# Reordering the mixers of the first block: the 16-token tile second, output slots divided by tokens, rotations and value turn moved up

## What is computed

```
z = h @ w_in[l]
c_q, c_kv, k_pe, rq, rk, rv, rg = jnp.split(z, split_idx, axis=-1)
y_mla = mla_mixer(c_q, c_kv, k_pe, ...)       # latent attention, 4 heads of 128
y_ret = retention_mixer(rq, rk, rv, rg, ...)  # retention, 4 heads of 128
y = jnp.concatenate([y_mla, y_ret], axis=-1) @ w_out[l]
h_res = h_res + y
```

```
bounds = [0] + [N_META + BLOCK * j for j in range((L - N_META) // BLOCK + 1)]   # 0, 16, 144, 272
s = einsum('bqhd,bkhd->bhqk', qb, kb) * scale;  s = where(causal, s, -1e30)
p = softmax(s);  o = p @ vb                      # then rms_norm(o) per head
```

## Time and profile before

| | us |
|---|---|
| median of 3 runs (2362.45 to 2374.36) | 2368.86 |
| the profiled execution | 2357.2 |
| its span | 2355.5 |
| PE busy | 2254.0 |
| DVE busy | 1445.8 |
| ACT busy | 837.7 |

### The profile page before, as it was taken

The page is one execution under the profiler, slowest core; times in us unless marked ns, Lnnn a source line. Parts: engine busy times, 40 slices in busy tenths (PEclk is TensorE's granted clock), DMA queues, the critical chain, the costliest instruction groups (busy, mean ns, idle before and its releaser), DMA issues. The chain is left out here.

```text
span 2355.5 us, 36541 instructions
## 1 busy us (share of the span) xinstructions
PE 2254.0 (96%) x13794; PEld 2025.9 (86%) x13794; DVE 1445.8 (61%) x2239; ACT 837.7 (36%) x1139; POOL 142.9 (6%) x217
## 2 busy tenths in 40 slices
PE   7988999998999899999999999999999999989998
PEld 7878999987999788888888888898888888758998
DVE  4646776555777777678778767773333354386555
ACT  4334334334534422122342222242212233365433
POOL 1110000010000000000000001000000000000000
PEclk9988999999999999999999999999999999999999
DMA  5324675322566455555336546433233233203453
GB/s 213 107 72 140 206 235 187 135 77 96 199 232 199 158 197 181 181 181 173 122 117 205 179 165 199 159 111 99 87 107 107 74 105 110 88 19 125 170 187 125
DMA packets 65431, 343.14 MB, mean 146 GB/s; under 512 B 7105, under 2 KB 10433, under 8 KB 42561
## 3 DMA queue, kind: packets, MB, share of 16 engines
q1 hardware_dynamic: 44608, 266.47, 33.2%
q0 software_dynamic: 20736, 75.51, 10.1%
HBM read 340.90 MB, written 1.05 MB: 145 GB/s over the span
## 5 line engine op out<-in xcount | busy, mean ns | idle before, releaser
L703 PE MATMUL gpt<-xn_hi,w_hi 128*128 128x512 f32 (+2 forms) x2480 | 825.9, 333 | 6.3 <-DVE w_lo L1659 3.3
L704 PE MATMUL gpt<-xn_lo,w_hi 128*128 128x512 f32 (+2 forms) x2480 | 822.2, 332 | 0.0
L705 PE MATMUL gpt<-xn_hi,w_lo 128*128 128x512 f32 (+2 forms) x2480 | 822.2, 332 | 0.0
L1659 DVE TENSOR_TENSOR w_lo<-raw,w_hi 128x2048 fp32r<-128x2048 f32 (+3 forms) x282 | 573.1, 2032 | 271.8 <-ACT w_hi L1238 270.4
L1238 ACT ACTIVATE w_hi<-raw 128x2048 fp32r<-128x2048 f32 (+3 forms) x282 | 480.0, 1702 | 392.3 <-PE gpt L705 327.8
L703 PEld LDWEIGHTS gpt<-xn_hi,w_hi 128*128 128x128 f32 x2480 | 469.2, 189 | 50.9 <-DVE w_lo L1659 4.0
L704 PEld LDWEIGHTS gpt<-xn_lo,w_hi 128*128 128x128 f32 x2480 | 469.4, 189 | 43.3
L705 PEld LDWEIGHTS gpt<-xn_hi,w_lo 128*128 128x128 f32 x2480 | 469.4, 189 | 43.1
L703 PE MATMUL gpt<-mid_hi,w_hi 128*128 128x512 f32 (+2 forms) x996 | 333.2, 335 | 1.7 <-DVE w_lo L1659 1.0
L704 PE MATMUL gpt<-mid_lo,w_hi 128*128 128x512 f32 (+2 forms) x996 | 332.3, 334 | 0.0
L705 PE MATMUL gpt<-mid_hi,w_lo 128*128 128x512 f32 (+2 forms) x996 | 332.3, 334 | 0.0
(11 more groups left out here) (284 smaller groups left out, 2156.9 us busy)
## 6 DMA issues: line engine op xcount, KB each, us to landing
raw<-in_up_a SPq DMA_DIRECT2D x72, 1024.0 KB, 4.8
ada_w<-in_ada POOLq DMA_DIRECT2D x144, 512.0 KB, 3.7
raw<-in_up_b SPq DMA_DIRECT2D x60, 1024.0 KB, 4.8
raw<-in_down_a SPq DMA_DIRECT2D x48, 768.0 KB, 4.2
raw<-in_down_b SPq DMA_DIRECT2D x48, 640.0 KB, 3.9
raw<-in_win SPq DMA_DIRECT2D x16, 1024.0 KB, 4.9
raw<-in_qkv SPq DMA_DIRECT2D x12, 1024.0 KB, 4.8
raw<-in_wout SPq DMA_DIRECT2D x8, 1024.0 KB, 4.8
```

The source lines that it names most:

```text
L703: mm(o, w_hi[b][:, j, :], hi(k), start=(k == 0), stop=False)
L704: mm(o, w_hi[b][:, j, :], lo(k), start=False, stop=False)
L705: last = mm(o, w_lo[b][:, j, :], hi(k), start=False, stop=(k == kt - 1))
L1659: V.tensor_tensor(w_lo[b][:, 0:tiles, :], raw[b][:, 0:tiles, :], w_hi[b][:, 0:tiles, :].bitcast(F32), ALU.subtract).then_inc(lo_ready, 1)
```

## The change

1. **Rotations moved up.** In the projections DVE does rotations 6 and 7 before the split of the next slot.
2. **Value turn moved up.** `v_turn(1)` stands before `gate(1)`; on ACT its copies (`v_evac(1)`) stand before the retention's squares.
3. **The 16-token tile second.** `m_tiles` is (2, 0, 1) for L = 0: tile 0 goes ahead of tile 1 everywhere. Banks are given out anew (`MO`, `MO_T`), and `m_square(2)` on ACT stands before `m_pt(1)`.
4. **Output slots divided by tokens.** Over k = 0 to 3 a slot is now done in two pieces, `out_tokens(b, 2)` for the 128 tokens of tile 2 and `out_tokens(b, 1)` for the tokens before them (144 at L = 0, 128 at L = 1). The piece of tile 2 runs while tile 1 is still being worked on. `mo_hi` and `mo_lo` are now counted per head. The retention's pieces are spread out more: k = 6, k = 7 apart, and slot 1's k = 6, 7 at the very end.
5. **The third slot's split in halves** (`split_halves`): the first 8 of 16 tiles are rounded and subtracted first, and PE's first half of the slot waits for them alone (`gemm(..., early=L + 1)`).

```diff
-        MO_T = [mb[3], mb[2], mb[0]]
-        MO = [mb[1], mb[2], mb[3]]
+        MO = [mb[2], mb[0], mb[3]]
+        MO_T = [[mb[2], mb[2]], [mb[0], mb[1]], [mb[3], mb[1]]]
...
-            return (2, 1, 0) if L == 0 else (2, 1)
+            return (2, 0, 1) if L == 0 else (2, 1)
...
                 gate(0, second, k_thin)
-                gate(1, range(KT))
...
                 v_turn(1)
+                gate(1, range(KT))
...
+                def out_tokens(b, q):
+
+                    first = MTOK[2][0] - c0
+                    a = slice(first, n) if q == 2 else slice(0, first)
+                    for k in range(HEADS):
+                        if b == 0:
+                            pe.wait_ge(mo_lo, HEADS * turn_of(L, q) + k + 1)
+                        for m in range(2):
+                            o = gp[b][m][:, a]
+                            j = m * KT + k
+                            mm(o, w_hi[b][:, j, :], hi(k)[:, a], start=False, stop=False)
+                            mm(o, w_hi[b][:, j, :], lo(k)[:, a], start=False, stop=False)
+                            last = mm(o, w_lo[b][:, j, :], hi(k)[:, a], start=False, stop=(b == 0 and q == 1 and k == HEADS - 1))
...
-                m_turn(1)
-                m_pv(1)
                 if L == 0:
                     m_turn(0)
-                out_part(0, (6, 7))
+                m_turn(1)
+                out_part(0, (6,))
                 if L == 0:
                     m_pv(0)
+                m_pv(1)
+                out_part(0, (7,))
                 mo_turn(2)
-                out_part(1, (4, 5, 6, 7))
-                mo_turn(1)
+                out_part(1, (4, 5))
                 if L == 0:
                     mo_turn(0)
-                pe.wait_ge(mo_lo, turn_of(L, m_tiles(L)[-1]) + 1)
-                for b in range(2):
-                    out_part(b, (0, 1, 2, 3)).then_inc(slot_done, 1)
-                for b in range(2):
-                    gemm(pl + S_OUT // 2 + 1, b, KT, 2, hi, lo, n)
+                out_tokens(0, 2)
+                mo_turn(1)
+                out_tokens(1, 2)
+                out_tokens(0, 1).then_inc(slot_done, 1)
+                out_tokens(1, 1)
+                out_part(1, (6, 7)).then_inc(slot_done, 1)
+                gemm(pl + S_OUT // 2 + 1, 0, KT, 2, hi, lo, n, early=L + 1)
+                gemm(pl + S_OUT // 2 + 1, 1, KT, 2, hi, lo, n)
...
+            def split_halves(p, b):
+
+                act.wait_ge(raw_in[b], p * 16 + 16)
+                act.wait_ge(slot_done, free_at(2 * p + b))
+                A(w_hi[b][:, 0:KT, :], raw[b][:, 0:KT, :], ACT.Copy).then_inc(first_hi, 1)
+                A(w_hi[b][:, KT:SIDE_T, :], raw[b][:, KT:SIDE_T, :], ACT.Copy).then_inc(hi_ready, 1)
...
                 for s in range(4, 8):
-                    nxt(s)
+                    if s < 7:
+                        nxt(s)
                     for k in (2 * s - 8, 2 * s - 7):
                         rope(L * ROPES1, k, rope1(k), T1, rot_a, rot_b, ROT)
+                    if s == 7:
+                        nxt(s)
...
                 m_y(2)
+                if L == 0:
+                    m_mean(0)
                 m_mean(1)
-                m_y(1)
                 m_lo(2)
                 if L == 0:
-                    m_mean(0)
+                    m_y(0)
+                m_y(1)
+                if L == 0:
+                    m_lo(0)
                 m_lo(1)
```

More of the change, by code:

```diff
@@ L688, in gemm_first, with gemm @@
                     last.then_inc(slot_done, 1)
-            def gemm(p, b, kt, mt, hi, lo, n, ready=None, r0=0):
+            def gemm(p, b, kt, mt, hi, lo, n, ready=None, r0=0, early=None):
                 s = 2 * p + b
@@ L694, in gemm @@
                     pe.wait_ge(ready, r0 + kt - 2)
-                pe.wait_ge(lo_ready, done_at(s))
+                if early is None:
+                    pe.wait_ge(lo_ready, done_at(s))
+                else:
+                    pe.wait_ge(first_lo, early)
                 pe.wait_ge(evac_done, free_at(s))
                 for m in range(mt):
+                    if m == 1 and early is not None:
+                        pe.wait_ge(lo_ready, done_at(s))
                     o = gp[b][m][:, 0:n]
@@ L951, in m_turn @@
                         for h in range(HEADS):
-                            last = nc.tensor.transpose(mb[1 if q == 0 else j][0:ks, h * tn_:(h + 1) * tn_],
+                            last = nc.tensor.transpose(mb[2 if q == 0 else j][0:ks, h * tn_:(h + 1) * tn_],
                                                        prob[q][0:tn_, h, t0:t0 + ks], ident[0:tn_, 0:tn_])
@@ L971, in mo_turn @@
                     for h in range(HEADS):
-                        last = nc.tensor.transpose(MO_T[q][:, h * tn_:(h + 1) * tn_], mo[q][0:tn_, h * P:(h + 1) * P],
+                        last = nc.tensor.transpose(MO_T[q][h // 2][:, h * tn_:(h + 1) * tn_], mo[q][0:tn_, h * P:(h + 1) * P],
                                                    ident[0:tn_, 0:tn_])
@@ L1006, in out_part @@
                             mm(o, w_hi[b][:, j, :], lo(k), start=False, stop=False)
-                            last = mm(o, w_lo[b][:, j, :], hi(k), start=False, stop=(k == HEADS - 1))
+                            last = mm(o, w_lo[b][:, j, :], hi(k), start=False, stop=(b == 1 and k == KT - 1))
+                    return last
+                def out_tokens(b, q):
[10 more added lines that the diff above has]
+                            last = mm(o, w_lo[b][:, j, :], hi(k)[:, a], start=False, stop=(b == 0 and q == 1 and k == HEADS - 1))
                     return last
@@ L1440, in m_pt @@
                         ks = MTOK[j][1]
-                        last = A(turned[q][j][0:ks, 0:HEADS * tn_], mb[1 if q == 0 else j][0:ks, 0:HEADS * tn_], ACT.Copy)
+                        last = A(turned[q][j][0:ks, 0:HEADS * tn_], mb[2 if q == 0 else j][0:ks, 0:HEADS * tn_], ACT.Copy)
                     last.then_inc(mla_pt, 1)
@@ L1454, in m_hi @@
                     for h in range(HEADS):
-                        last = A(xn_hi[:, h, t0:t0 + tn_], MO_T[q][:, h * tn_:(h + 1) * tn_], ACT.Identity,
-                                 scale=lv[:, V_MO + h:V_MO + h + 1])
-                    last.then_inc(mo_hi, 1)
+                        A(xn_hi[:, h, t0:t0 + tn_], MO_T[q][h // 2][:, h * tn_:(h + 1) * tn_], ACT.Identity,
+                          scale=lv[:, V_MO + h:V_MO + h + 1]).then_inc(mo_hi, 1)
                 m_exp(2)
@@ L1895, in out_slots @@
                         residual(s0 + g, 2 * g + m, b, m, m == 1)
-                    if g < 3 and tiles[g] is not None:
+                    if g == 0 and early is not None:
+                        split_halves(p + 1, b, early)
+                    elif g < 3 and tiles[g] is not None:
                         split(p + 1, b, tiles[g])
```

56 lines of the change are left out of this document (31 added, 25 removed).

## The result

| | before | after |
|---|---|---|
| median, us | 2365.65 (4 runs, 2356.77 to 2374.36) | 2340.30 (4 runs, 2338.08 to 2346.71) |
| ratio, 95% interval | | 0.9904 [0.9879, 0.9928] |
| profiled execution, us | 2357.2 | 2346.7 |
| its span, us | 2355.5 | 2345.0 |
| PE busy, us | 2254.0 | 2263.1 |

The kernel is faster by 22.7 us by the ratio, 17 to 29. The two profiled executions stand only 10.5 us apart: the one of after is the slowest of its four runs. A second set of 8 runs of the same kernel gave 0.9932 [0.9908, 0.9955]; the mean over all 12 runs is 2346.4 against 2364.5 over 68 runs of the kernel before, 18.1 us less.

A forecast was written before the change was run, and what follows sets the result against it. PE, busy for 96% of the span, bounds the kernel; time is won only where it idles or runs slowly. 5.9 + 3.3 + 10.4 - 7.2 + 5.0 = 17.4 off 2368.9 gives 2351.5; forecast alone 2340 to 2360, 8-in-10 range to 2369.

The forecast's parts named there:

- Rotations: At the value turn 0: waits of 4.4 us go and 1.5 us of half clock is won, 5.9 us gained.
- Value turn: At the value turn 1: copies run under gate 1's products, so the keys' norms' rows start at once, 3.3 us gained.
- C: Rival at gate 1: the moved value turn keeps the clock down, costing 3.2 us, so 2354.7; chance 12%.
- The Trainium skill's rule on transposes: At the moved value turn: transposes don't count as PE-busy for the clock gate, by which the 12% rival would come true.
- The tail's idle time: In the tails of both layers: PE's waits shrink or go, 1.9 + 3.9 + 2.6 + 2.0 = 10.4 us gained.
- D: Rival in the tail: DVE and ACT set its length, so the waits stay; gain 7.0, 2361.9; chance 10%.
- The divided products: In the tail: 96 divided products at 0.10 us replace 48 wide ones costing 6.0 a layer, 7.2 us lost in all.
- The Trainium skill's 81 ns for 128 columns: Alternative price of a divided product in the tail, by which the 192 would cost 3.6 us less; not adopted.
- A: Rival in the tail: narrow fp32r products take four passes, 0.226 us each, 24.2 us more, so 2375.7; chance 12%.
- B: Rival in the tail: divided products run at half clock, 0.175 us each, 14.4 us more, so 2365.9; chance 18%.
- The tail's clock: In both tails: with idle pieces gone, half of the 9.9 us lost to low clock is won back, 5.0 us gained.
- the part on how the changed profile would look: Signs: no waits at turns or third slot, 0.09 to 0.11 us a divided product, about 1 us for `m_y(0)`.

The follow-up runs named there:

- turn_only: The kernel before with only the value turn 1 and its copies on ACT moved up; median 2358.08 us, ratio to before 0.9981.
- tail_only: The changed kernel with rotations and value turn put back, so only the tail differs from the kernel before; median 2351.54 us, ratio to before 0.9962.
- div64: The changed kernel with every divided product cut in two, 64 columns and the rest; median 2403.79 us, ratio to before 1.0167.
- rot_only: The kernel before with only rotations 6 and 7 moved ahead of the split; median 2357.72 us, ratio to before 0.9979.
- filler_only: The kernel before with only slot 1's products over k = 6 and 7 moved between the transposes of tiles 1 and 0; 2367.59 us, ratio 0.9995.
- after_again: The changed kernel itself, unaltered, in a second set of 8 runs; median 2347.80 us, ratio to before 0.9932.
- no_halves: The changed kernel with the third slot's split whole again, all else kept; median 2345.85 us, ratio to before 0.9918.
- div_slot0: The changed kernel with the division by tokens kept for slot 0 alone; median 2342.28 us, ratio to before 0.9900.

## Why the prediction was right

Forecast 2351.5, from 2368.9 less 17.4; measured 2340.3, and 18.1 us less over all runs. The 11.2 us between forecast and measurement are nearly all of the starting points: 2368.9, a median of three runs, was 4.4 us above the mean of 68, and the four runs of after, with a good clock (0.9815 against 0.9779 in the next eight), have a median 6.1 us below the mean of all 12. By its steps:

- **Rotations, 5.9 forecast:** 4.9 at equal clock. The idle time of 4.4 went in full. The 1.5 of clock is too small for the mean clock to show; the half-clock pieces at the turn, 5 in 8 cases with the wait and 0 in 20 without it, are 2.1 us in the mean of a kernel and speak for it.
- **Value turn, 3.3 forecast:** 4.1. Both waits went. **C**, that the turn keeps the clock down, did not come: turn_only gained, with the mean clock as before. The Trainium skill's rule on transposes, quoted with C, is neither borne out nor refuted by the piece behind the turn, since pieces like it come and go with the turn in either place.
- **The tail's idle time, 10.4 forecast:** 10.4 at full clock. The waits in the tail were 1.15 + 3.17 + 1.55 + 1.39 in layer 0 and 0.39 + 1.15 + 2.39 + 1.18 in layer 1, 12.4 in all; in tail_only 1.15 + 0.39 + 0.44 = 2.0 are left, with `m_y(0)` as forecast (1.2). In the first profile of after 1.2 are left, as its PE came late to `m_y(0)` at half clock. **D** did not come.
- **The divided products, 7.2 loss forecast:** 9.7. The term that was mis-sized is the price: 0.1115 in place of 0.10. 96 of them cost 10.7 us a layer; 48 whole ones cost 6.05 with 272 columns and 5.65 with 256 (three in 0.353 us behind 558.12 in the changed profile). The row behind the 0.10, 0.093 for a sum, was misread without harm: rows 8 show two sums of two instructions each, so 0.093 is an instruction with its load. 10.4 - 9.7 = 0.7 is, within its error of 1.0, what tail_only shows at equal clock (1.3). The Trainium skill's 81 ns for 128 columns, quoted in the prediction, was off by more. Its figure for loading weights does fit at full clock: the Trainium skill ("TensorE: Matmul & The Clock Gate", section on LDWEIGHTS) gives the columns of the weights / 1.2 in ns, with no term for the moving operand. For 128 that is, as an estimate, 107; 64, 128 and 144 columns all cost 0.112 here. It doesn't fit at half clock, where div64 shows 0.213. **A** (0.22) is refuted. **B** did not come either: in the ten tails with 128 or 144 columns a product (five profiles) the clock stayed full over all of them. Had it not, its price of 0.175 may have been too kind: div64's pieces, narrower ones, cost 0.213 at half clock, and there what B feared for the clock did come.
- **The tail's clock, 5.0 forecast:** 7.7, from tail_only's mean clock, give or take 4.4. I had counted 9.9 us of loss in both tails and there were 12.0, since the piece from 171.0 to 174.3 was left out; 1.4 of the 12.0 are idle time. Over the four unchanged tails (before, rot_only, turn_only, filler_only) the loss is 10.2 to 12.0; over the five with the change's tail or half of its division (after, after_again, tail_only, no_halves, div_slot0) 0 to 5.1, 2.7 in the mean. So it wins some three quarters of it, not half. Half was a guess between nothing and all, with no mechanism behind it.

5.9 + 3.3 + 10.4 - 7.2 + 5.0 = 17.4 was forecast; 4.9 + 4.1 + 1.3 + 7.7 = 18.0 is what the parts measured. The two errors that were larger than 1 us, the price (2.5) and the clock (2.7), have opposite signs, so it is luck that the sum came within 1 us. Of the part on how the changed profile would look, these held: no wait at the turns and the third slot; 0.11 a product; 1.1 us for `m_y(0)` where the clock is full. PE at half clock in the two tails, forecast as 10 us where there were 20, was 3.4 in after, 10.2 in after_again and 0 in tail_only, where before had 23.9.

What the prediction did not see is that one of the change's five parts, the division, costs more than it gives. Taken out, with slot 1's last pieces as filler, it leaves a kernel 7 us faster at equal clock, 2337.2 and 2335.6 us in the median of its two sets.

## What to carry to other kernels

A gap is best filled with work that has to be done anyway, in its full width. Cutting a product in two by tokens doubles the loads of weights, and in these pieces the load is the price (0.112 us for 64, 128 or 144 columns, against 0.126 for the whole 272): ask what whole piece can be moved into the gap before dividing one.

Compare small edits at equal clock. Where a run lists its granted clock, a line through all runs turned 0.21% of scatter (4.9 us over the 68 runs of before) into 0.06%, and showed which part of a gain is work and which is clock.

## What the hardware showed that I had not expected

- In div64 the clock fell to 1.2 GHz 3.4 us (layer 0) and 5.6 us (layer 1) into a stream of fp32r products with 64 to 80 columns, and stayed there for all the rest of it, 35 and 31 us, and 6 and 3 us into the whole products behind, though PE was busy throughout. Streams of 128 and 144 columns, at the same 0.112 us each, ran at 2.4 GHz in all ten tails that have them (7 to 11 us each). The Trainium skill ("TensorE: Matmul & The Clock Gate", part on the clock gate, section on what is happening) says that the clock goes by how busy PE has been; PE's busy time in these rows, 41.00 of 41.00, does not tell the two apart. Why the clock fell stays open.
- At half clock a piece of 64 columns costs 0.213 us, as much as a whole product of 256 columns there (layer 1 of div64, behind 610.56). By these two prices a whole product cut in narrow pieces costs twice as much where the clock is low.
- One kernel's clock differs from execution to execution at the same place: over the sums of layer 0 the changed kernel lost 8.5 us in one profile and 6.8 in the next, and its variants 1.7 to 8.5.
